# A transformer block chain on one core: two norms in a row from one set of sums, roots by token, and the first products behind them row by row

## The reference, cut to what matters

```python
def layer_norm(x):
    mu = jnp.mean(x, -1, keepdims=True)
    var = jnp.mean(jnp.square(x - mu), -1, keepdims=True)
    return (x - mu) * lax.rsqrt(var + EPS)

x = layer_norm(ALPHA * x + g1 * (mix @ w_out)) * ln1_g + ln1_b      # "p1"
u = layer_norm(x) * (1 + sc2) + sh2                                 # "f", into ffn_w_up
x = layer_norm(ALPHA * x + g2 * (act @ w_down)) * ln2_g + ln2_b     # "p2"
xn = x * lax.rsqrt(mean(x * x) + EPS) * g_mix                       # "g0", into w_in_2
```

## Time and profile before

| | us |
|---|---|
| median of three runs | 2193.51 (2193.3 to 2193.61) |
| the profiled execution | 2194.71 |
| its span, first to last instruction | 2192.9 |
| TensorE busy | 2095.1 (96%), mean granted clock 0.975 |
| VectorE, ScalarE, GpSimd busy | 1164.2, 894.5, 776.3 |

### The profile page before, as it was taken

One profiled execution on the slowest core, in us unless ns is written; L12 is line 12 of the kernel. 1 busy time (PEld: TensorE's weight loads), 2 busy tenths in 40 slices (PEclk: granted clock), 3 DMA queues, 4 the chain that ended last, 5 costly groups with the idle time before them and its releaser, 6 DMA issues. The chain is left out here.

```text
span 2192.9 us, 25628 instructions
## 1 busy us (share of the span) xinstructions
PE 2095.1 (96%) x10218; PEld 1596.0 (73%) x10218; DVE 1164.2 (53%) x1966; ACT 894.5 (41%) x1405; POOL 776.3 (35%) x397
## 2 busy tenths in 40 slices
PE   6999988999999799999999999989999999999999
PEld 3877746888887377767888888667765678888866
...
DMA packets 186662, 194.21 MB, mean 89 GB/s; under 512 B 8497, under 2 KB 181937, under 8 KB 186161
## 3 DMA queue, kind: packets, MB, share of 16 engines
...
## 5 line engine op out<-in xcount | busy, mean ns | idle before, releaser
L2553 POOL TENSOR_TENSOR wl<-ring,wh 128x1024 fp32r<-128x1024 f32 (+1 forms) x253 | 621.8, 2462 | 1025.7 <-ACT wh L1315 1024.3
L1315 ACT ACTIVATE wh<-ring 128x1024 fp32r<-128x1024 f32 (+2 forms) x294 | 304.3, 1043 | 355.7 <-PE ps L786 275.5
L784 PE MATMUL ps<-xh,wh 128*128 128x512 f32 x992 | 390.9, 394 | 6.9 <-DVE xl L1860 6.9
L785 PE MATMUL ps<-xl,wh 128*128 128x512 f32 x992 | 388.3, 391 | 0.0
L786 PE MATMUL ps<-xh,wl 128*128 128x512 f32 x992 | 388.1, 391 | 0.0
L786 PE MATMUL ps<-acts,wl 128*128 128x512 f32 x880 | 351.0, 399 | 0.0
L784 PE MATMUL ps<-acts,wh 128*128 128x512 f32 x880 | 347.8, 395 | 3.1 <-DVE wl L1822 3.1
L785 PE MATMUL ps<-acts,wh 128*128 128x512 f32 x880 | 348.1, 396 | 0.0
L2204 DVE SCALAR_TENSOR_TENSOR mix<-ps,par,mix 128x441 f32<-128x441 f32 (+2 forms) x352 | 214.1, 688 | 40.1 <-ACT mix L1528 40.1
L784 PEld LDWEIGHTS ps<-xh,wh 128*128 128x128 f32 x992 | 187.2, 189 | 52.6 <-issue 11.2
L786 PEld LDWEIGHTS ps<-xh,wl 128*128 128x128 f32 x992 | 187.4, 189 | 39.3
(11 more groups left out here) (366 smaller groups left out, 3039.6 us busy)
## 6 DMA issues: line engine op xcount, KB each, us to landing
...
```

Source lines behind the costliest of these rows:

```text
L784: t.matmul(b[0:m, 0:n], s.hi[:, k, a:a + m], x2[0][:, k, :], start=k == ks[0], stop=False)
L785: t.matmul(b[0:m, 0:n], s.hi[:, k, a:a + m], x2[1][:, k, :], start=False, stop=False)
L1315: a.activation(s.hi[:, :, c], s.ap[:, :, c], ACT.Copy).then_inc(*up("hi", "hi", name, hf))
L2553: p.tensor_tensor(s.lo[:, :, c], s.ap[:, :, c], s.hi[:, :, c].bitcast(F32), ALU.subtract).then_inc(*up("lo_pool", "lo", name, hf))
```

## The change

While the last stage of a seam still runs, `ahead_of_norm` forms on TensorE a mean of the first four tiles alone, doubled, as a shift; VectorE subtracts it as tiles arrive, and two matmuls a row (`sums`) gather six sums by token: of x, of x times two weight vectors, of x squared plain and weighted with the gain squared. `gains` prepares those vectors and their totals. `statistics` turns the sums so that tokens lie on the partitions (`tS`), computes both norms' means and variances there on 128x4 tiles, and `spread` brings one number a token back to all partitions. GpSimd subtracts what the shift left (`centered`). Seam one: three VectorE operations a row and the low half; the first four products run together, row by row. Seam two: the same, with four `tok.0` products together, and no sums for `g0`. The norm ahead of layer 1 gets its root and reciprocal by token.

```diff
@@ -1046,6 +1056,60 @@
+def ahead_of_norm(tag, j, row):
+    if j in (1, 3):
+        i = j // 2
+        b = take(("tot", tag, i))
+        e.wait_ge(*at("gain", tag, i))
+        t.matmul(b[:, 0:24 - 8 * i], cc("mean"), (wt[:, 512:536], wt[:, 536:552])[i]).then_inc(*full(("tot", tag, i)))
+    if j == 4:
+        b = take(("rows", tag))
+        for n in range(4):
+            e.wait_ge(*taken(row(n)))
+            i = t.matmul(b[32 * n:32 * n + 32, :], cc("mean", 32), h[:, n, :])
+        i.then_inc(*full(("rows", tag)))
+    if j == 5:
+        b = take(("mean", tag), keep=True)
+        e.wait_ge(*taken(("rows", tag)))
+        t.matmul(b[:, :], cc("fold"), partf).then_inc(*full(("mean", tag)))
+    if j == 6:
+        take(("parts", tag), keep=True)
+        sums(tag, (0, 1))
+    if j == 7:
+        sums(tag, range(2, 8))
+def sums(tag, rows):
+    b = ps(("parts", tag))
+    for j in rows:
+        o = 32 * (j % 2)
+        e.wait_ge(*at("W", tag))
+        e.wait_ge(*(at("shifted", tag, j) if j < 7 else taken(("mean", tag))))
+        t.matmul(b[o:o + 32, :], W1[:, j, :], mix[:, j, :], start=j < 2, stop=j >= 6)
+        e.wait_ge(*at("sq", tag, j))
+        i = t.matmul(b[64 + o:96 + o, :], W2[:, j, :], sqf[j % 4], start=j < 2, stop=j >= 6)
+        i.then_inc(*(up("read", "sqread", tag, j) if j < 7 else full(("parts", tag))))
+def statistics(tag, where=(None, None, None)):
+    banks.drop(("mean", tag))
+    banks.drop(("parts", tag))
+    b = take(("tS", tag), where=where[0])
+    e.wait_ge(*taken(("parts", tag)))
+    for c in range(4):
+        i = t.matmul(b[:, 8 * c:8 * c + 8], partf[:, c * 128:c * 128 + 128], cc("pair", 8))
+    i.then_inc(*full(("tS", tag)))
+    spread(("dl", tag), st[:, :, 0], at("st", tag), where=where[1])
+    spread(("R1", tag), inv1, at("r1", tag), keep=where[2] is None, where=where[2])
+def spread(key, src, wait, keep=False, where=None):
+    b = take(key, keep, where)
+    e.wait_ge(*wait)
+    for c in range(4):
+        i = t.matmul(b[:, c * 128:c * 128 + 128], src[:, c:c + 1].to_broadcast([128, 128]), ident)
+    i.then_inc(*full(key))
@@ -1053,22 +1117,42 @@
-mean("p1", h, T, lambda j: taken(("wout", j)), partf)
-squares("p1", sqf, T, partf)
-mean("f", h, T, lambda j: at("hn", "p1", j), partf)
-squares("f", sqf, T, partf)
+    ahead_of_norm("p1", j, lambda n: ("wout", n))
+statistics("p1")
+spread(("m2", "p1"), st[:, :, 4], at("m2", "p1"), keep=True)
+spread(("R2", "p1"), inv2, at("r2", "p1"), keep=True)
...
+    if g == 0:
+        first = [(kind, 0, jl) for jl in range(2) for kind in ("ug", "uv")]
+        for key in first:
+            use(key, (key[0], 0, 0), (key[2],), who="pool")
+            take(key, keep=True)
+        for k in range(8):
+            e.wait_ge(*at("xl", "f", k))
+            for key in first:
+                s, c = W.named[key[0], 0, 0], slice(128 * key[2], 128 * key[2] + 128)
+                e.wait_ge(*at("lo", s.name, key[2]))
+                t.matmul(ps(key)[:, :], s.hi[:, k, c], xh[:, k, :], start=k == 0, stop=False)
+                t.matmul(ps(key)[:, :], s.hi[:, k, c], xl[:, k, :], start=False, stop=False)
+                i = t.matmul(ps(key)[:, :], s.lo[:, k, c], xh[:, k, :], start=False, stop=k == 7)
+                if k == 7:
+                    i.then_inc(*full(key))
+        for what in ("R1", "m2", "R2"):
+            banks.drop((what, "p1"))
...
-            product((kind, g, jl), (kind, g, jl // 2), jl % 2, (xh, xl), xk=("xl", "f"), who="pool", keep=True)
+            if g or jl >= 2:
+                product((kind, g, jl), (kind, g, jl // 2), jl % 2, (xh, xl), xk=("xl", "f"), who="pool", keep=True)
...
+        if g == 2:
+            ahead_of_norm("p2", j, lambda n: ("dn", 2, n))
@@ -1076,15 +1160,11 @@
-mean("p2", h, T, lambda j: taken(("dn", 2, j)), partf)
-squares("p2", sqf, T, partf)
-b = take(("parts", "g0"))
-for j in range(8):
-    square("g0", j, b, sqf)
+statistics("p2", (3, 5, 7))
...
@@ -1150,14 +1230,40 @@
-            fold(("var", f"g{l}"), ("parts", f"g{l}"), partf if l == 0 else layers[0].part, where=where[0])
+            if l:
+                key = ("var", "g1")
+                b = take(key, where=where[0])
+                e.wait_ge(*taken(("parts", "g1")))
+                for c in range(4):
+                    j = t.matmul(b[:, 2 * c:2 * c + 2], layers[0].part[:, c * 128:c * 128 + 128], cc("pair", 2))
+                j.then_inc(*full(key))
...
-            turn(key, [small[0:1, c * 128:c * 128 + 128] for c in range(4)], at("rs", f"g{l}"), w=1, where=where[0])
+            spread(key, n.rsT, at("rsI", l), where=where[0])
+        elif kind == "tok" and (l, k[0]) == (0, 0):
+            if k[1] == 0:
+                s = W.named["tok", 0, 0]
+                first = [(("tok", 0, 0, c), w) for kd, (i, c), (w,) in
+                         [p for p in layer["tensor"] if p[0] == "tok"] if i == 0]
+                for key, w in first:
+                    use(key, s.name, (0, 1), key[3] == 3, 0)
+                    take(key, where=w)
+                for hf in range(2):
+                    e.wait_ge(*at("lo", s.name, hf))
+                for i in range(8):
+                    e.wait_ge(*at("xl", "g0", i))
+                    for key, w in first:
+                        x0, x1 = [x[:, i, key[3] * 128:key[3] * 128 + 128] for x in (xh, xl)]
+                        t.matmul(ps(key)[:, 0:256], x0, s.hi[:, i, :], start=i == 0, stop=False)
+                        t.matmul(ps(key)[:, 0:256], x0, s.lo[:, i, :], start=False, stop=False)
+                        j = t.matmul(ps(key)[:, 0:256], x1, s.hi[:, i, :], start=False, stop=i == 7)
+                        if i == 7:
+                            j.then_inc(*full(key))
@@ -1334,8 +1440,28 @@
...
+def ahead_of_norm(tag, j, high):
+    if j == 3:
+        a.activation(roots[:, 0:1], eps[:, 0:1], ACT.Sqrt).then_inc(*up("act"))
+    if j == 5:
+        rows_of(("rows", tag), partf, scale=2.0)
+    if j in (6, 7):
+        for n in ((0, 1, 2, 3), (4, 5, 6))[j - 6]:
+            square(tag, n, mix[:, n, :], sqf, at("shifted", tag, n))
+    if j == 7:
+        high()
+        square(tag, 7, mix[:, 7, :], sqf, taken(("mean", tag)))
+def statistics(tag):
+    rows_of(("parts", tag), partf, scale=1.0 / 1024)
+    e.wait_ge(*at("var1", tag))
+    a.activation(roots[:, 0:4], st[:, :, 2], ACT.Sqrt, bias=eps[:, 0:1]).then_inc(*up("act", "root1", tag))
+    rows_of(("dl", tag), rsf)
+    e.wait_ge(*at("var2", tag))
+    a.activation(roots[:, 4:8], var_f, ACT.Sqrt, bias=eps[:, 0:1]).then_inc(*up("act", "root2", tag))
@@ -1494,21 +1620,17 @@
+for j in range(7):
+    high(("wout", j))
+    ahead_of_norm("p1", j, None)
+ahead_of_norm("p1", 7, lambda: high(("wout", 7)))
+statistics("p1")
+high(("ug", 0, 0))
...
-    high(("wout", j))
...
-    if i == 0:
-        for j in range(8):
-            e.wait_ge(*at("scaled", tag, j))
-            a.activation(h[:, j, :], h[:, j, :], ACT.Identity, bias=pc(b, j)).then_inc(*up("act", "hn", tag, j))
-e.wait_ge(*done(("wout", 7)))
-shifted("f", mix, xh, lambda j: mod3[:, 24 + j, 0:1])
-for j in range(8):
-    a.activation(h[:, j, :], h[:, j, :], ACT.Copy, scale=ALPHA).then_inc(*up("act", "h1", j))
+    e.wait_ge(*(at("scaled", "f", j) if j < 7 else taken(("R2", "p1"))))
+    a.activation(xh[:, j, :], mix[:, j, :], ACT.Identity, bias=mod3[:, 24 + j, 0:1]).then_inc(*up("act", "xh", "f", j))
+    a.activation(h[:, j, :], h[:, j, :], ACT.Identity, bias=ab[:, j:j + 1], scale=ALPHA).then_inc(*up("act", "h1", j))
+high(("uv", 0, 0))
@@ -1543,7 +1666,10 @@
-high(("dn", g, j))
+if (g, j) != (2, 7):
+    high(("dn", g, j))
+    if g == 2:
+        ahead_of_norm("p2", j, None)
@@ -1554,22 +1680,20 @@
-rows_of(("rows", "p2"), partf)
-squares("p2", mix, T, sqf, lambda j: center("p2", j))
-rows_of(("parts", "p2"), partf)
-root("p2", rsf)
+ahead_of_norm("p2", 7, lambda: high(("dn", 2, 7)))
+statistics("p2")
+for c in range(4):
+    high(("tok", 0, 0, c))
...
-    e.wait_ge(*at("scaled", "p2", j))
+    e.wait_ge(*(at("scaled", "p2", j) if j < 7 else taken(("R1", "p2"))))
...
+    feed("g0", j, at("hn", "p2", j), ("g_mix_2", 0), sqf, xh, done(("uv", 2, 5)), mine=False)
...
@@ -1846,6 +1974,76 @@
+def gains(tag, g, b, step, centered):
+    G, B = pc(g, 0, 8), pc(b, 0, 8)
+    if step == 0:
+        v.tensor_copy(gq[:, 0, :], B).then_inc(*up("vec"))
+        v.tensor_copy(gq[:, 1, :], G).then_inc(*up("vec"))
+        v.tensor_tensor(gq[:, 2, :], G, G, ALU.mult).then_inc(*up("vec", "gain", tag, 0))
+        v.memset(wt[:, 0:512], 0.0).then_inc(*up("vec"))
...
+    elif step == 1:
+        e.wait_ge(*done(("tot", tag, 0)))
+        v.tensor_reduce(gk[:, 0:3], ps(("tot", tag, 0))[:, 0:24].rearrange("p (i j) -> p i j", i=3), X, ALU.add).then_inc(*free(("tot", tag, 0)))
+        e.wait_ge(*taken(("tot", tag, 0)))
...
+        v.tensor_tensor(gq2[:, 0, :], G, b1, ALU.mult).then_inc(*up("vec", "gain", tag, 1))
```

(103 more changed lines are left out.)

82 lines of the change are left out of this document (54 added, 28 removed).

## The result

| | us |
|---|---|
| before, median of four runs | 2193.4 (2190.6 to 2193.6) |
| changed, median of four runs | 2160.1 (2155.7 to 2164.8) |
| ratio | 0.985, 95% interval 0.983 to 0.988 |
| the profiled execution of the changed kernel, its span | 2158.4, 2156.4 |
| TensorE busy, mean granted clock | 2076.0 (96%), 0.980 |

33.3 us were gained where 35.8 were forecast. Waits of TensorE over the whole span (total, times, longest), the answer to the earlier trace rows: seven waits for GpSimd's squares (14.2) are gone, what is left of the seams is short.

What follows compares the result with a forecast made beforehand. TensorE, busy 96% of the span, bounds the kernel, so only its waits and lower-clock time can be won. 13.9 (seam one) + 22.7 (seam two) - 0.8 (layer 1) = 35.8 us, taking the median 2193.5 to 2157.7; range 2146 to 2176.

Steps and rivals of the forecast that it cites:

- likeliest branch: The main forecast, 65%: both seams gain, layer 1 loses a little, 35.8 us in sum, median 2157.7.
- Added work: Partial mean, sums, fold and totals on TensorE before the last wout and dn products: 3.5 us a seam, bounds 3 to 6.
- The tail as a chain: Seam one, behind the last wout matmul: square, weight halves, low halves, eviction, last sums in sequence; sums at 8.8 us.
- Statistics: Seam one: copying, turning and spreading the sums by token; dl copied 13.2 us after the last wout matmul starts.
- The fourth product's half: Seam one: low half of the fourth product's weight tile, taken by GpSimd only behind all eight subtractions, ready at 329.0.
- The clock in the group: Seam one's four row-by-row products: full clock back at 330.4, then seven rows at 2.72 us, to 349.3.
- The wait in front of the fifth product: Seam one: the fifth product's weight half can be rounded only when the first product is complete; TensorE waits 1.6 us.
- VectorE's lag: First up stage, behind the fifth product: VectorE late by up to 9.7 us; nothing booked, bounds 0 to 9.7.
- rival of late weights: VectorE's lag in the first up stage is paid after all, 8 us more, 2166; chance 12%.
- The port: By the exclusive-lock rule, VectorE low halves beside GpSimd could cost some 1 us more a row for five rows.
- Seam two: From the dn stage through the tok.0 group and 80-column products: 24.9 us gained, less 2.2 for lower clock, 22.7.
- Layer 1: Norm ahead of layer 1: four small turns and a spread replace a fold and transposes; 0.8 us dearer, 0.3 to 1.2.

Runs made afterwards that it cites:

- e5: Changed kernel with the four 256-column tok.0 products of seam two run one behind the other instead of row by row together; seam one untouched: 2161.1 us.
- e2: Changed kernel with ScalarE rounding the two weight halves due at the last wout product ahead of squares 4 to 6 instead of behind them: 2151.5 us, ratio 0.982.
- e3: Changed kernel with the fourth product's weight half rounded behind the copy of the sums, its low half taken by GpSimd before the eight subtractions: 2159.5 us, ratio 0.985.

## Why the prediction was right, and where it was not

2157.7 was predicted, 2160.1 measured, inside 2146 to 2176, and on the likeliest branch. One reading was loose: the waits named first are not the two longest of the kernel. Among those between the 14.2 and the 6.9 us of the earlier trace rows are one for the input `x` (11.1) and one at L1207 (10.6), which the change doesn't touch (10.8 and 10.0 after). By its steps:

- **Added work, 3.5 each.** In `wout` 4.1 by the starts of the last matmul (302.85 against 298.74), 4.3 with the 0.2 by which the changed kernel led before; in the `dn` stages 3.2 (344.47 against 341.31 from the fifth product to the last `dn` matmul). Inside the bounds; the only wait in either is one of 0.2 us at the start of `wout`.
- **The tail as a chain.** Right in every link; 9.5 us where I had 8.8, because the clock fell in the wait for the last tile and the last passes took 1.06. With a later fall it was 8.6 (e5), and e2 shows the price of the chain, 5.7.
- **Statistics.** `dl` at 14.8 for 13.2; 12.1 at the full clock. The bounds for turns and spreads, one to 1.9 us, took it in; here both sat at the dear end.
- **The fourth product's half.** Found, and too early by 2.4 (331.4 for 329.0): GpSimd started its subtractions 2.1 late and took 1.35 a row for my 1.30. Of this 0.6 was the added work, which had moved everything behind it.
- **The clock in the group** is the step that failed: "here at 330.4" and then full for good. It came back ahead of the group and fell twice more, in front of and behind the wait for the fourth product's half. Counted from the last `wout` matmul, row 0 ended 1.4 us late (29.4 for 28.0), behind that late half, and the seven other rows took 20.8 us for 19.0. So the fifth product is 3.2 us later than forecast by the table (51.9 against 48.7), and with the 0.6 of added work seam one gave 10.1 us where 13.9 were booked. e5, with the same program in the seam and a mean clock of 0.89 for 0.84, beat the forecast of the table by 1.0.
- **The wait in front of the fifth product**, 1.6 forecast: 1.7. **VectorE's lag**, booked at nothing: TensorE has no other wait from 354 to 600. The rival of late weights did not occur.
- **The port.** Beside subtractions the low halves of seam one lost 0.13 and 0.04 us, of seam two 0.37. Beside the low half of a weight tile VectorE stood until GpSimd was through: L2364 ended at 331.94, 0.55 behind it, and in e3 a small operation 0.02 behind it, while L2360, which reads PSUM, took its usual 0.75. The rule of the Trainium skill (SBUF — State Buffer, "SBUF: two separate sides") describes these two rows, roughly; the rows beside subtractions, two in seam one and five in seam two, paid far less than the 1 us that I had worked out by it.
- **Seam two.** 22.7 forecast; 71.6 to 44.8 us from the last `dn` matmul to the wide product, less the 3.2 of added work, is 23.6. First product at 13.5 (13.2 forecast), group's end at 27.4 (27.4). The clock fell 4.4 us into the 80-column stretch, not 3.4. That VectorE, not TensorE, paces rows at the full clock didn't show, since the lower clock hid it.
- **Layer 1**, -0.8 forecast: from the copy of its sums to the first 80-column matmul 13.71 us against 13.35, 0.4 dearer.
- **Layer 1's mixer** helps to explain why the profile (36.5 gained for 35.8) agrees better than the medians (33.3): there the clock's stretches fall differently from run to run (305.3 and 309.6 for one program). I had no term for it, and no bound. Of the difference 1.3 us is on the other side, since the profiled execution before took 2194.7 for a median of 2193.4; where the changed kernel's other runs spent their time no trace shows. Two misses of about 3 us, seam one's and this one, cancelled in the first profile: that it agrees to 0.7 us is luck.

Not settled: 0.5 us of lead that the loads show behind seam one (10.6) and the starts of the fifth product don't (10.1); and what makes the clock fall a moment earlier in one run than in another.
